# Attention and state-space encoder on one core: norm sums placed inside the input projection, head 0 prepared in separate banks, gate projection ended bank by bank

## The chip, the core and the metric
The kernel is one program on one core of one Trainium2 chip. The metric is the device time in microseconds of one execution. The core has TensorE for matrix products, whose results land in PSUM (eight banks of 512 f32 columns on 128 partitions), VectorE, ScalarE and GpSimd for everything else, and SyncE for most DMA issues. An engine takes its instructions in the order written; engines wait for each other by semaphores.

## The reference
An encoder with two layers runs over two sequences of 528 tokens (16 of them shared meta tokens), width 1024. Layer 0 mixes by attention with low-rank keys, values and queries, layer 1 by a chunked state-space scan; a gated feed-forward part follows each. The change touches these parts:

```python
def mla_mixer(u, w_in, q_norm, kv_norm, w_q_up, w_kv_up, q_head_norm, k_head_norm, w_out):
    c_q, c_kv, k_rope = jnp.split(u @ w_in, [Q_LORA_RANK, Q_LORA_RANK + KV_LORA_RANK], axis=-1)
    q = (rmsnorm(c_q, q_norm) @ w_q_up).reshape(b, L, MLA_HEADS, QK_HEAD_DIM)
    kv = (rmsnorm(c_kv, kv_norm) @ w_kv_up).reshape(b, L, MLA_HEADS, QK_NOPE_DIM + V_HEAD_DIM)
    k_nope, v = jnp.split(kv, [QK_NOPE_DIM], axis=-1)
    k = jnp.concatenate(
        [k_nope, jnp.broadcast_to(k_rope[:, :, None, :], (b, L, MLA_HEADS, QK_ROPE_DIM))], axis=-1)
    q, k = rmsnorm(q, q_head_norm), rmsnorm(k, k_head_norm)
    q, k = apply_rope(q, pos), apply_rope(k, pos)
    o = block_attention(q, k, v)
    return o.reshape(b, L, MLA_HEADS * V_HEAD_DIM) @ w_out

def ssd_mixer(u, w_in, conv_w, conv_b, dt_bias, a_log, d_skip, norm_w, w_out):
    z, xbc, dt_raw = jnp.split(u @ w_in, [D_INNER, D_INNER + CONV_DIM], axis=-1)
    ...
    y = y.reshape(b, L, D_INNER) * jax.nn.silu(z.astype(jnp.float32))
    y = rmsnorm(y, norm_w).astype(u.dtype)
    return y @ w_out
```

There are 16 heads with 64 plain and 32 rotated dimensions; the query rank is 384, the key-value rank 256. `z` has 2048 columns.

## The kernel before
All products are made in three parts: operand and weight are each split in a high and a low part (`Uhi`, `Ulo`, `Whi`, `Wlo`), and high x high, high x low and low x high are added in PSUM. GpSimd splits the weights (`Whi`, `Wlo`), two slots of them, one unit ahead of TensorE.

**Input projection (L852 to L858).** Six blocks of 128 output rows (m = 0 to 2 for the query rank, 3 and 4 for the key-value rank, 5 for the rotated key) go in turn to the bank groups 0 to 2 and 3 to 5. `product` runs eight steps (kt) of nine multiplications for each. ScalarE copies each block out, writes its high part and its squares; VectorE writes the low part and adds up the squares (`add_squares`, L1952) into SS for the input, SSQ[0] for the query rank and SSQ[1] for the key-value rank.

**Norm sums (L859 to L866).** Behind the projection TensorE sums the squares over the partitions by ten multiplications with one column each (`sums_by_part`, L826), four sets: SS, SSQ[0], SSQ[1] and the rotated key's squares SQ. VectorE then makes the norm factors of all tokens (TOK) in a chain of 45 small operations (L2032 to L2044), which ends with a signal `row_ready`. In between TensorE does the rotated key's pair product (L867 to L870, three multiplications of 352 columns), which gives it with its halves exchanged.

**Head 0 (L1024 to L1070).** Every product of the preparation uses one pair of banks, A_PREP = 5 and 6, and waits (`wait_prep`) until the engine that empties it has done so. The order is: two spreads of the rope factors over the partitions, K of both sequences, then the loop over j from -1 on. Its pass j = -1 has no scores, and prepares head 0 as each pass j >= 0 prepares head j + 1 between its own scores: Q (18 multiplications of 264 columns for each sequence), sums for the key norms and query norms, V in four parts (`V_PARTS`, 60 multiplications of 256 columns in all), two spreads of key factors. `prep_orders` numbers the uses of the pair, and ScalarE and VectorE count by these numbers (`prep_taken`, `stats_taken`). ScalarE empties Q and half of K and makes high parts; VectorE makes the factors, scales, turns the queries and makes low parts.

**Gate projection (L1272 to L1300).** Layer 1's `z` is made in four groups of 512 columns. A group fills all eight banks, one for each window of 128 tokens (w), over eight steps kt, two of them in each weight unit q:

```python
for kk in range(2):
    kt = 2 * q + kk
    for w in range(WIN):
        if kt == 0 and group_:
            pe.wait_ge(z_taken, (group_ - 1) * WIN + w + 1)
```

Each bank gets its last multiplication in the last step, and ScalarE empties the banks from 0 to 7 (`take_gates`, L1786 to L1795) by a Silu, ZB, which a DMA stores. Ahead of group 2 TensorE makes cumulative sums in banks 5 to 7, and ahead of group 3 exponent rows in banks 6 and 7; both wait for all eight banks. So does the scan that follows (L1304): its first products go to bank 5 (`products_bc`, tiles CCH and BCH), then to banks 0 to 3 (`decays`, tiles RH and LHS) and bank 4 (`chunk_state`, tiles XW and BTOK).

Every multiplication that is not a score or an output product is recorded with line L748, where the helper `mm` stands, so groups are told apart by their tiles.

## Time and profile before

| | us |
|---|---|
| median of three runs | 3419.45 |
| lowest and highest | 3417.31, 3433.54 |
| the profiled execution | 3425.27 |
| its span | 3423.5 |

| engine | busy, share of the span | instructions |
|---|---|---|
| PE (TensorE multiplications) | 3263.1 us, 95% | 19150 |
| PEld (weight loads) | 2945.2 us, 86% | 19150 |
| DVE (VectorE) | 1793.5 us, 52% | 2388 |
| ACT (ScalarE) | 791.0 us, 23% | 1395 |
| POOL (GpSimd) | 1258.4 us, 37% | 570 |

The mean granted clock of TensorE is 0.967 of its full 2.4 GHz; a stretch shows either 1.00 or 0.50, or a mixture where it holds both. Times of rows count from the start of the span. In a timeline a row is a run of like instructions: its start, its length, engine, line, operation, what it writes and reads, its shape and count, and in brackets the idle time of the engine before it, with what ended that.

### The profile page before, as it was taken

Reading aid. Unit: us, or ns where it says so; the run is one execution under the profiler, and the core shown is the slowest. Engines: PE = TensorE matmul, PEld = TensorE weight load, DVE = VectorE, ACT = ScalarE, POOL = GpSimd, SP = SyncE. Lnnn points to the kernel's source line nnn. Section 1 sums busy time; section 2 is a strip of 40 time slices with the busy share of each in tenths; the row PEclk is TensorE's granted clock in tenths of the full one; section 3 lists DMA queues with packets and bytes.
Section 4 is the critical chain, followed back from the end, with each engine's and each line's share of the span. In section 5 each row is a group of like instructions: output and inputs, shape, how many; then the busy total and the mean of one; then the engine's idle time right before and its main releaser. Section 6 shows DMA issues by size and latency. Waiting matters only on the chain.

```text
span 3423.5 us, 47898 instructions
## 1 busy us (share of the span) xinstructions
PE 3263.1 (95%) x19150; PEld 2945.2 (86%) x19150; DVE 1793.5 (52%) x2388; ACT 791.0 (23%) x1395; POOL 1258.4 (37%) x570
## 2 busy tenths in 40 slices
PE   7899999989999999999999999789998999999996
PEld 7799999989999999999999977566666788888885
DVE  4466666564333333334788842478888533333335
ACT  4165555461100000001211111233333100000001
POOL 4000000003444444444444343367673444444441
PEclk9699899899999999999999999899999999999998
DMA  2000000002111111111233422332323111111111
GB/s 107 19 12 9 14 5 14 14 19 82 44 43 43 47 45 43 45 47 44 92 93 93 134 74 99 103 103 92 110 92 111 43 48 44 49 44 48 49 47 57
DMA packets 112656, 198.66 MB, mean 58 GB/s; under 512 B 7413, under 2 KB 56821, under 8 KB 112501
## 3 DMA queue, kind: packets, MB, share of 16 engines
q1 hardware_dynamic: 71728, 146.82, 13.5%
q10 hardware_dynamic: 40773, 49.69, 4.3%
q8 instruction: 107, 1.75, 0.2%
q14 instruction: 48, 0.39, 0.0%
HBM read 161.10 MB, written 35.39 MB: 57 GB/s over the span
## 4 chain that ended last, share of the span: by engine, by line
PE 83%; DVE 7%; POOL 4%; issue 3%; ACT 2%; ACTq 1%; DMA 0%; DVEq 0%; POOLq 0%
PE PS L748 76%; PE PS L1019 4%; PE PS L1004 2%; POOL Wlo L669 1%; POOL SQ L714 1%; DVE SS L2261 1%; POOL RMS L679 1%; ACT ZB L1793 1%; DVE YC L2404 1%; PE PS L1209 1%; DVE SS L1952 0%; DVE H L2298 0%; DVE MX L2161 0%; PE PS L1346 0%; POOL SQ L709 0%
## 5 line engine op out<-in xcount | busy, mean ns | idle before, releaser
L626 POOL TENSOR_TENSOR Whi<-Wraw,const 128x1024 fp32r<-128x1024 f32 x186 | 451.7, 2428 | 1900.8 <-PE PS L748 1893.9
L748 PE MATMUL PS<-Uhi,Whi 128*128 128x352 f32 (+1 forms) x2504 | 620.3, 347 | 30.9 <-DVE Ulo L1964 19.3
L748 PE MATMUL PS<-Ulo,Whi 128*128 128x352 f32 (+1 forms) x2504 | 615.9, 346 | 0.0
L748 PE MATMUL PS<-Uhi,Wlo 128*128 128x352 f32 (+1 forms) x2504 | 614.3, 345 | 0.0
L629 POOL TENSOR_TENSOR Wlo<-Wraw,Whi 128x1024 fp32r<-128x1024 f32 x186 | 507.1, 2726 | 14.6
L748 PEld LDWEIGHTS PS<-Uhi,Whi 128*128 128x128 f32 x2504 | 440.1, 190 | 67.5 <-issue 18.7
L748 PEld LDWEIGHTS PS<-Ulo,Whi 128*128 128x128 f32 x2504 | 441.5, 189 | 31.3
L748 PEld LDWEIGHTS PS<-Uhi,Wlo 128*128 128x128 f32 x2504 | 440.8, 189 | 31.5
L2298 DVE TENSOR_TENSOR H<-H,PS 128x1056 f32<-128x1056 f32 (+1 forms) x176 | 217.5, 1237 | 264.8 <-PE PS L748 264.7
L2322 DVE TENSOR_TENSOR HID<-PS,RMS 128x1056 f32<-128x1056 f32 (+1 forms) x44 | 54.6, 1241 | 420.7 <-PE PS L748 420.2
L1703 ACT ACTIVATE HIDhi<-HID 128x1056 fp32r<-128x1056 f32 (+1 forms) x40 | 43.0, 1075 | 894.5 <-DVE HID L2327 894.5
L748 PE MATMUL PS<-HIDhi,Whi 128*128 128x352 f32 (+1 forms) x800 | 205.9, 355 | 5.3 <-DVE H L2298 5.3
L748 PE MATMUL PS<-HIDlo,Whi 128*128 128x352 f32 (+1 forms) x800 | 205.8, 355 | 0.0
L748 PE MATMUL PS<-HIDhi,Wlo 128*128 128x352 f32 (+1 forms) x800 | 205.7, 354 | 0.0
L2161 DVE TENSOR_REDUCE MX<-PS 106x1 f32<-106x528 f32 x160 | 113.1, 707 | 139.6 <-PE PS L748 138.3
L2404 DVE SCALAR_TENSOR_TENSOR YC<-XC,cols,YC 128x1052 f32<-128x1052 f32 (+1 forms) x96 | 180.8, 1883 | 3.4
L1019 PE MATMUL PS<-V,PT 106*106 106x64 f32 x1600 | 178.0, 261 | 0.5 <-ACT O L1605 0.5
L1019 PEld LDWEIGHTS PS<-V,PT 106*106 106x106 f32 x1600 | 170.4, 181 | 0.6 <-issue 0.6
L748 PEld LDWEIGHTS PS<-HIDhi,Whi 128*128 128x128 f32 x800 | 143.3, 190 | 20.7 <-DVE H L2298 6.0
L748 PEld LDWEIGHTS PS<-HIDlo,Whi 128*128 128x128 f32 x800 | 143.2, 190 | 14.9
L748 PEld LDWEIGHTS PS<-HIDhi,Wlo 128*128 128x128 f32 x800 | 142.9, 189 | 14.3
L2309 DVE TENSOR_TENSOR GATE<-PS,RMS 128x1056 f32<-128x1056 f32 (+1 forms) x43 | 53.4, 1241 | 191.1 <-PE PS L748 175.7
(288 smaller groups left out, 5369.0 us busy)
## 6 DMA issues: line engine op xcount, KB each, us to landing
Wraw<-in_w SPq DMA_DIRECT2D x211, 512.0 KB, 3.5
xt<-XTT ACTq DMA_DIRECT2D x20, 640.0 KB, 5.6
H<-in_x ACTq DMA_DIRECT2D x16, 528.0 KB, 7.9
Wraw<-in_w SPq DMA_DIRECT2D x32, 256.0 KB, 3.2
zt<-ZB ACTq DMA_DIRECT2D x32, 256.0 KB, 2.0
X<-xt SPq DMA_DIRECT2D x8, 1024.0 KB
Z<-zt SPq DMA_DIRECT2D x32, 256.0 KB, 2.6
saved<-H ACTq DMA_DIRECT2D x8, 528.0 KB, 7.4
```

The costliest lines, as they stand in the source:

```text
L626: pool.tensor_tensor(Whi[s][:], Wraw[s][:], ones.unsqueeze(1).broadcast_to([P, BLK, P]), ALU.mult)\
L629: pool.tensor_tensor(Wlo[s][:], Wraw[s][:], Whi[s][:].bitcast(F32), ALU.subtract)\
L669: pool.tensor_tensor(Wlo[s][:], Wraw[s][:], Whi[s][:].bitcast(F32), ALU.subtract)\
L748: ins = pe.matmul(out, lhsT, rhs, start=start, stop=stop, skip_group_check=True)
L1004: ins = pe.transpose(PS[0:CW, A_TURN + b // TURN_DVE, b % TURN_DVE * CW:(b % TURN_DVE + 1) * CW], PR[t % 2][:, key_start(b):key_start(b) + ...
L1019: ins = pe.matmul(PS[0:CW, A_OUT, 0:VD], PT[t % 2][:, b, :], V[x // 4 % 2][:, n // KB * KB + b, x // 2 % 2, x % 2 * VD:(x % 2 + 1) * VD], ...
L1703: act.activation(hi[:, k, 0:n], HID[:, 0:n], ACT.Copy).then_inc(hid_hi, c.adds(hid_hi))
L2161: step(vec.tensor_reduce(MX[:, t % RING:t % RING + 1], PS[0:CW, A_SCORE:A_SCORE + 2, 0:QHALF], AX_XY, ALU.max))
L2298: ins = vec.tensor_tensor(h, h, of(g), ALU.add)
L2309: vec.tensor_tensor(parted(GATE[:]), of(g), rms, ALU.mult)\
L2322: vec.tensor_tensor(parted(HID[:]), of(g), rms, ALU.mult)\
L2404: ins = vec.scalar_tensor_tensor(y_[:, :, to], x[:, :, of], taps[:, tap:tap + 1], y_[:, :, to], ALU.mult, ALU.add)
```

## The change
It has three parts.

**Norm sums.** The sets for SS, SSQ[0] and SSQ[1] are issued within the products of the fourth, fifth and sixth block (m = 3 and kt 0, m = 4 and kt 0, m = 5 and kt 4), in banks 6 and 7 in turn. VectorE's chain is cut: the part for the input norm stands in its loop behind block 2, the parts for query and key-value rank behind blocks 3 and 4. The tables of the rotation are loaded at the start, `trig_q` to its place and `trig_k` to the second half of KR, and `trig_q` is scaled behind block 0.

**Head 0.** Its preparation stands ahead of the loop, which begins with j = 0. K goes to banks 0, 1 and 2, 3; the rotated key's sums to bank 7; the pair product to banks 4 to 6; Q to banks 0, 1 and 2, 3; the rope spreads to 4, 5 and 2, 3; V to 6, 7, then 3, 4 and 2, 3, and 5, 6; the key spreads to 4, 5 and 0, 1. Five new semaphores carry what the counted uses carried. ScalarE's and VectorE's parts are written out in the same order.

**Gate projection.** The last unit of each group is done window by window, both steps of a window together, in the order 5, 6, 7, 0, 1, 2, 3, 4; ScalarE empties in that order. The waits for all eight banks become waits for the banks needed.

```diff
+ZORDER = (5, 6, 7, 0, 1, 2, 3, 4)
...
-    prep, stats = [("rope", s) for s in both] + [("k", 0, s) for s in both], []
-    for j in range(-1, HEADS - 1):
+    prep = [("k", 0, s) for s in both] + [("q", 0, s) for s in both] + [("v", 0, 0)]
+    prep += [("ks", 0, s) for s in both] + [("v", 0, i) for i in range(1, len(V_PARTS))]
+    stats = [("k", 0), ("q", 0)]
+    for j in range(HEADS - 1):
...
-    trig_k = RMS[:, 0:L]
+    trig_k = KR[1][:, 0:L]
...
+            def norm_sums(kt):
+                if (m, kt) in ((KQ, 0), (KQ + 1, 0), (KQ + KKV, 4)):
+                    k = m - KQ
+                    pe.wait_ge(sum_ready, c.want(sum_ready))
+                    sums_by_part(STAT_BANK + k % 2, k, (SS, *SSQ)[k], one).then_inc(stat_full, c.adds(stat_full))
+
+            product(group(m % 2), range(KD), Uhi, Ulo, range(KD), u_ready if m == 0 else None, norm_sums)\
                 .then_inc(to_scalar[m % 2], c.adds(to_scalar[m % 2]))
-        pe.wait_ge(sum_ready, c.want(sum_ready))
-        sums_by_part(STAT_BANK, 0, SS, one)
-        pe.wait_ge(sum_ready, c.want(sum_ready))
-        sums_by_part(STAT_BANK, 1, SSQ[0], one)
-        pe.wait_ge(sum_ready, c.want(sum_ready))
-        sums_by_part(STAT_BANK, 2, SSQ[1], one)
-        pe.wait_ge(rope_sq, c.want(rope_sq))
-        sums_by_part(STAT_BANK, 3, SQ, mask(M_ROPE)).then_inc(stat_full, c.adds(stat_full))
-        pe.wait_ge(rope_ready, c.want(rope_ready))
-        pe.wait_ge(grp_free[0], c.want(grp_free[0]))
-        for n in range(NB):
-            ins = mm(group(0)[:, n, :], pair_sum, CF[0][:, n * NT:(n + 1) * NT])
-        ins.then_inc(to_scalar[0], c.adds(to_scalar[0]))
         pe.wait_ge(u_ready, c.want(u_ready, KQ + KKV))
-        pe.wait_ge(row_ready, c.want(row_ready))
...
-        for g in range(2):
-            pe.wait_ge(grp_free[g], c.ahead(grp_free[g]))
+        pe.wait_ge(grp_free[0], c.ahead(grp_free[0]))
+        project_k(0, 0, 0)
+        pe.wait_ge(grp_free[1], c.ahead(grp_free[1]))
+        project_k(0, 1, 2)
+        pe.wait_ge(rope_sq, c.want(rope_sq))
+        sums_by_part(STAT_BANK + 1, 3, SSQ[1], mask(M_ROPE)).then_inc(stat_full, c.adds(stat_full))
+        pe.wait_ge(rope_ready, c.want(rope_ready))
+        for n in range(NB):
+            ins = mm(PS[:, 4 + n, 0:NT], pair_sum, CF[0][:, n * NT:(n + 1) * NT])
+        ins.then_inc(pair_full, 1)
+        pe.wait_ge(row_ready, c.want(row_ready))
+        key_norms(0, 0)
+        key_norms(0, 1)
         for s in range(NSEQ):
-            wait_prep("rope", s)
-            spread(s, TOK[:, K_RB, :])
-        for s in range(NSEQ):
-            project_k(0, s)
-        for j in range(-1, HEADS):
+            pe.wait_ge(prep_taken, PREP["k", 0, s] + 1)
+            pe.wait_ge(kr_taken, s + 1)
+            project_q(0, s, 0, 2 * s)
+            project_q(0, s, 1, 2 * s)
+        pe.wait_ge(pair_taken, 1)
+        spread(pair(4), 0, TOK[:, K_RB, :]).then_inc(rope_full, 1)
+        pe.wait_ge(prep_taken, PREP["q", 0, 1] + 1)
+        spread(pair(2), 1, TOK[:, K_RB, :]).then_inc(rope_full, 1)
+        project_v(0, 0, 6)
+        pe.wait_ge(rope_taken, 1)
+        spread_keys(0, 0, 4)
+        spread_keys(0, 1, 0)
+        query_norms(0, 0)
+        query_norms(0, 1)
+        pe.wait_ge(rope_taken, 2)
+        project_v(0, 1, 3)
+        project_v(0, 2, 2)
+        pe.wait_ge(prep_taken, PREP["ks", 0, 0] + 1)
+        project_v(0, 3)
+        for j in range(HEADS):
...
+        def z_matmul(w, kk, kt):
+
+            t = slice(window_start(w), window_start(w) + CK)
+            for p, (Xs, W) in enumerate(((Uhi, Whi), (Uhi, Wlo), (Ulo, Whi))):
+                ins = mm(PS[:, w, :], Xs[:, kt, t],
+                         W[now["slot"]][:, kk * HALF:(kk + 1) * HALF, :].rearrange("p m n -> p (m n)"),
+                         start=(kt == 0 and p == 0), stop=(kt == KD - 1 and p == 2))
+            return ins
+
+        def z_taken_from(group_, bank):
+
+            return group_ * WIN + ZORDER.index(bank) + 1
+
         for group_ in range(GROUPS):
             if group_ == 2:
-                pe.wait_ge(z_taken, 2 * WIN)
+                pe.wait_ge(z_taken, z_taken_from(1, 7))
                 cumulative_sums()
             if group_ == 3:
-                pe.wait_ge(z_taken, 3 * WIN)
+                pe.wait_ge(z_taken, z_taken_from(2, 7))
                 exponent_rows()
             for q in range(KD // 2):
                 enter_unit(V_Z + group_ * TILES_PER_GROUP + q)
+                if q == KD // 2 - 1:
+                    for w in ZORDER:
+                        z_matmul(w, 0, 2 * q)
+                        z_matmul(w, 1, 2 * q + 1).then_inc(z_full, 1)
+                    continue
                 for kk in range(2):
-                    kt = 2 * q + kk
                     for w in range(WIN):
-                        if kt == 0 and group_:
-                            pe.wait_ge(z_taken, (group_ - 1) * WIN + w + 1)
+                        if q == 0 and kk == 0 and group_:
+                            pe.wait_ge(z_taken, z_taken_from(group_ - 1, w))
                             if group_ == 2 and w > 4:
                                 pe.wait_ge(tab_taken, w - 4)
                             if group_ == 3 and w > 5:
                                 pe.wait_ge(rows_taken, 1)
-                        t = slice(window_start(w), window_start(w) + CK)
-                        for p, (Xs, W) in enumerate(((Uhi, Whi), (Uhi, Wlo), (Ulo, Whi))):
-                            ins = mm(PS[:, w, :], Xs[:, kt, t],
-                                     W[now["slot"]][:, kk * HALF:(kk + 1) * HALF, :].rearrange("p m n -> p (m n)"),
-                                     start=(kt == 0 and p == 0), stop=(kt == KD - 1 and p == 2))
-                        if kt == KD - 1:
-                            ins.then_inc(z_full, 1)
+                        z_matmul(w, kk, 2 * q + kk)
         now["release"], now["slot"] = now["slot"], None
-        pe.wait_ge(z_taken, GROUPS * WIN)
...
+        pe.wait_ge(z_taken, z_taken_from(3, 5))
         products_bc(0)
+        pe.wait_ge(z_taken, z_taken_from(3, 3))
         decays(0)
+        pe.wait_ge(z_taken, z_taken_from(3, 4))
         chunk_state(0, 0, 4)
...
+        for k in range(2):
+            act.dma_start(trig_q[:, k, :], trig_d[k]).then_inc(trig_in, 16)
...
+        act.activation(banks(CF[1][:]), group(1), ACT.Copy).then_inc(rope_raw, 1)
+        act.wait_ge(rope_raw, 1)
         act.sem_inc(grp_free[1], 1)
         act.wait_ge(sum_ready, c.want(sum_ready))
-        act.activation(SQ[:], CF[1][:], ACT.Square).then_inc(rope_sq, c.adds(rope_sq))
-        act.wait_ge(to_scalar[0], c.want(to_scalar[0]))
-        act.activation(banks(KR[0][NOPE:P, :]), group(0, parts=P - NOPE, at=NOPE), ACT.Copy)\
-            .then_inc(act_steps, c.adds(act_steps))
-        act.activation(banks(KR[1][0:P - NOPE, :]), group(0, parts=P - NOPE), ACT.Copy)\
-            .then_inc(grp_free[0], c.adds(grp_free[0]))
+        act.wait_ge(stat_full, c.want(stat_full, 3))
+        act.activation(SSQ[1][:], CF[1][:], ACT.Square).then_inc(rope_sq, c.adds(rope_sq))
         sq_by[0] = None
-        act.wait_ge(stat_full, c.want(stat_full))
-        for k in range(2):
-            act.dma_start(trig_q[:, k, :], trig_d[k]).then_inc(trig_in, 16)
-
-
-        halves = PS[:, A_PREP:A_PREP + 2, 0:QHALF]
+        c.want(stat_full)
...
+        for s in range(NSEQ):
+            take_k(0, s, 2 * s)
+        act.wait_ge(pair_full, 1)
+        act.activation(banks(KR[0][NOPE:P, :]), PS[NOPE:P, 4:7, 0:NT], ACT.Copy).then_inc(act_steps, c.adds(act_steps))
+        act.activation(banks(KR[1][0:P - NOPE, :]), PS[0:P - NOPE, 4:7, 0:NT], ACT.Copy).then_inc(pair_taken, 1)
+        for s in range(NSEQ):
+            take_q(0, s, 2 * s)
+        high_q(0)
+        high_k(0)
...
-            for w in range(WIN):
-                n = group_ * WIN + w
+            for i, w in enumerate(ZORDER):
+                n = group_ * WIN + i
...
+            if m == 0:
+                vec.wait_ge(trig_in, c.want(trig_in, 48))
+                for h in range(2):
+                    step(vec.tensor_scalar(trig_q[:, h, :], trig_q[:, h, :], col("q_head", h), None, ALU.mult))
+            if m == KQ - 1:
+                vec.wait_ge(stat_full, c.want(stat_full))
...
+            if m >= KQ:
+                k = m - KQ
+                rank, dst, dst2 = ((Q_RANK, K_A, K_A2), (KV_RANK, K_B, K_B2))[k]
...
+        step(vec.tensor_copy(tok(K_BV), tok(K_B)))
+        for w in range(KB - 1, KW, KB):
+            step(vec.tensor_tensor(TOK[:, K_BV, w:w + 1], TOK[:, K_B, w:w + 1], lower[0:CW, 2:3], ALU.mult))
+        vec.wait_ge(rope_raw, 1)
...
+        vec.wait_ge(rope_ready, c.given(rope_ready))
         for s in range(NSEQ):
-            scale_rope(s)
-        take_k(0, 0)
-        for j in range(-1, HEADS):
+            take_k(0, s, 2 * s)
+        vec.wait_ge(stat_full, c.want(stat_full))
+        step(vec.scalar_tensor_tensor(tok(K_RR), part_sum(STAT_BANK + 1, 3), 1.0 / QK, tok(K_R1SQ), ALU.mult, ALU.mult))
+        vec.sem_inc(row_ready, 1)
+        step(vec.tensor_scalar(tok(K_RR), tok(K_RR), EPS, None, ALU.add))
+        key_factors(0, 0)
+        key_factors(0, 1)
+        scale_rope(0, 4)
+        scale_rope(1, 2)
+        take_v(0, 0, 6)
+        turn_queries(0)
+        scale_keys(0, 0, 4)
+        scale_keys(0, 1, 0)
+        low_q(0)
+        low_k(0)
+        query_factors(0, 0)
+        take_v(0, 1, 3)
+        take_v(0, 2, 2)
+        query_factors(0, 1)
+        take_v(0, 3)
+        for j in range(HEADS):
```

Below, SS, SSQ and SQ are the sums of squares, CF the raw rotated key, TOK the factors by token, Chi and Clo the parts of the normed low-rank block.

TensorE, from the end of the input projection to the first products of head 0, before:

```order
L748 MATMUL PS<-const,SS 106x1 [waits sum_ready]
L748 MATMUL PS<-const,SS 106x1 x9
L748 MATMUL PS<-const,SSQ 106x1 [waits sum_ready]
L748 MATMUL PS<-const,SSQ 106x1 x9
L748 MATMUL PS<-const,SSQ 106x1 [waits sum_ready]
L748 MATMUL PS<-const,SSQ 106x1 x9
L748 MATMUL PS<-const,SQ 106x1 [waits rope_sq]
L748 MATMUL PS<-const,SQ 106x1 x9
L748 MATMUL PS<-CF,const 128x352 [waits grp_free0,rope_ready]
L748 MATMUL PS<-CF,const 128x352 x2
L748 MATMUL PS<-const,TOK 128x106 [waits grp_free0,grp_free1,row_ready,u_ready]
```

TensorE, from the last K product of head 0 to its first Q product, after:

```order
L757 MATMUL PS<-Clo,Whi 128x264 x2
L757 MATMUL PS<-Chi,Wlo 128x264 x2
L757 MATMUL PS<-const,SSQ 106x1 [waits rope_sq]
L757 MATMUL PS<-const,SSQ 106x1 x9
L757 MATMUL PS<-CF,const 128x352 [waits rope_ready]
L757 MATMUL PS<-CF,const 128x352 x2
L757 MATMUL PS<-const,SS 106x2 [waits k_squared,row_ready]
L757 MATMUL PS<-const,SS 106x2 x9
L757 MATMUL PS<-Chi,Whi 128x264 [waits kr_taken,prep_taken]
L757 MATMUL PS<-Chi,Whi 128x264
```

Three of the four sets of sums have left this place, K stands ahead of the remaining set and Q behind the key norms; the spreads come later and wait for `pair_taken` and `prep_taken` alone.

VectorE, at the fourth block of the projection, before:

```order
L2020 SCALAR_TENSOR_TENSOR Clo<-CF,cols,Chi 128x1056 [waits hi_ready]
L1952 TENSOR_TENSOR SSQ<-SSQ,SQ 128x1056 [waits sq_free,sq_full]
L2020 SCALAR_TENSOR_TENSOR Clo<-CF,cols,Chi 128x1056 [waits hi_ready]
L1949 COPY SSQ<-SQ 128x1056 [waits sq_full]
L2020 SCALAR_TENSOR_TENSOR Clo<-CF,cols,Chi 128x1056 [waits hi_ready]
L1952 TENSOR_TENSOR SSQ<-SSQ,SQ 128x1056 [waits sq_free,sq_full]
L2027 SCALAR_TENSOR_TENSOR CF<-CF,cols,RMS 128x1056 [waits u_ready,trig_in,rope_sq]
L2032 TENSOR_SCALAR TOK<-PS 106x10 [waits stat_full]
L1975 TENSOR_SCALAR TOK<-TOK 106x10 [waits vec_steps]
```

VectorE, at the third to the fourth block, after:

```order
L2065 SCALAR_TENSOR_TENSOR Clo<-CF,cols,Chi 128x1056 [waits hi_ready]
L1997 TENSOR_TENSOR SSQ<-SSQ,SQ 128x1056 [waits sq_free,sq_full]
L2074 TENSOR_SCALAR TOK<-PS 106x10 [waits stat_full]
L2020 TENSOR_SCALAR TOK<-TOK 106x10 [waits vec_steps]
L2023 TENSOR_SCALAR TOK<-TOK 106x10 [waits vec_steps]
```

The chain's first operation, which stood behind the rope product of CF, now stands behind the squares of the third block.

TensorE, where the gate projection ends and the scan begins, before:

```order
L748 MATMUL PS<-Whi,Ulo 128x512
L748 MATMUL PS<-CCH,BCH 128x128 [waits hg_in0,z_taken]
L748 MATMUL PS<-CCH,BCH 128x128 x3
L748 MATMUL PS<-RH,LHS 128x512 [waits rh_in0,hg_in0]
L748 MATMUL PS<-RH,LHS 128x512 x3
L748 MATMUL PS<-XW,BTOK 128x512 [waits xw_ready,hg_in0]
```

The same place, after:

```order
L757 MATMUL PS<-Whi,Ulo 128x512
L757 MATMUL PS<-CCH,BCH 128x128 [waits hg_in0,z_taken]
L757 MATMUL PS<-CCH,BCH 128x128 x3
L757 MATMUL PS<-RH,LHS 128x512 [waits rh_in0,hg_in0,z_taken]
L757 MATMUL PS<-RH,LHS 128x512 x3
L757 MATMUL PS<-XW,BTOK 128x512 [waits xw_ready,hg_in0,z_taken]
```

The order is the same; one wait for all banks has become three for the banks of each product.

## Rows read from the trace of the kernel before

**Rows 1.** Chain of waits, shares of the span by engine (part 4).
```profile
PE 83%; DVE 7%; POOL 4%; issue 3%; ACT 2%; ACTq 1%; DMA 0%; DVEq 0%; POOLq 0%
```

**Rows 2.** Timeline of TensorE, projection's end to scores: start, us, instructions.
```profile
93.86 1.94 PE L748 MATMUL PS<-const,SS 128*106 128x1 f32 x20
...
100.65 3.74 PE L748 MATMUL PS<-const,SQ 128*106 128x1 f32 x20
104.25 3.87 PE L748 MATMUL PS<-CF,const 128*128 128x352 f32 x6
...
165.99 0.56 PE L748 MATMUL PS<-KHI,QHI 128*106 128x264 f32 x2
```

**Rows 3.** Waits of TensorE, 94 to 166: total us, how many, longest.
```profile
PE PS L748 <- DVEq L2045: 5.6, 1, 5.6
PE PS L748 <- DVE KR L2069: 3.2, 2, 1.6
```

**Rows 4.** Windows, TensorE: stretch, length, busy (count), granted clock, DMA, GB/s.
```profile
113.70:142.40 28.70, 22.22 (x99) 0.50 0.06 19
142.40:149.20 6.80, 5.68 (x51) 1.00 0.00 0
```

**Rows 5.** Timeline of TensorE at the gate projection's four group borders.
```profile
2014.87 0.47 PE L748 MATMUL PS<-Whi,Uhi 128*128 128x512 f32 x1 [2.25 <-ACT ZB L1793]
...
2066.75 1.02 PE L748 MATMUL PS<-A,const 128*128 128x320 f32 x4 [3.91 <-ACT ZB L1793]
...
2121.56 1.45 PE L1269 MATMUL PS<-const,KT 128*128 128x128 f32 x8 [3.91 <-ACT ZB L1793]
...
2172.93 1.71 PE L748 MATMUL PS<-CCH,BCH 128*128 128x128 f32 x8 [3.91 <-ACT ZB L1793]
```

**Rows 6.** Windows, TensorE, columns as in rows 4.
```profile
872.90:876.30 3.40, 3.40 (x13) 0.50 0.48 154
...
2067.50:2074.30 6.80, 6.80 (x21) 0.50 0.11 41
2122.20:2125.50 3.30, 3.30 (x12) 0.50 0.21 79
...
374.00:397.80 23.80, 23.80 (x126) 0.51 0.01 2
```

**Rows 7.** Timeline of TensorE, first feed-forward part.
```profile
869.34 2.29 PE L748 MATMUL PS<-const,SS 128*128 128x1 f32 x20
```

**Rows 8.** Timeline of VectorE, additions of squares.
```profile
33.77 1.26 DVE L1952 TENSOR_TENSOR SS<-SS,SQ 128x1056 f32<-128x1056 f32 x1
...
86.11 3.44 DVE L1952 TENSOR_TENSOR SSQ<-SSQ,SQ 128x1056 f32<-128x1056 f32 x1
```

**Rows 9.** Timeline of VectorE, first and last of the 45 small operations.
```profile
104.43 0.17 DVE L2032 TENSOR_SCALAR TOK<-PS 106x10 f32<-106x10 f32 x1 [6.76 <-PE PS L748]
...
113.42 0.17 DVE L2044 SCALAR_TENSOR_TENSOR TOK<-PS,TOK 106x10 f32<-106x10 f32 x1
```

**Rows 10.** Chain that ended last: start, us, work (part of it).
```profile
113.75 2.88 PE PS L748 x12
...
127.30 2.99 PE PS L748 x12
...
131.88 11.36 PE PS L748 x56
...
149.68 2.87 PE PS L748 x12
...
160.74 5.46 PE PS L748 x24
```

**Rows 11.** Window, TensorE, third group of the gate projection; columns as in rows 4.
```profile
2140.00:2160.00 20.00, 20.00 (x88) 1.00 0.50 166
```

**Rows 12.** Timeline of ScalarE, first and last Silu of the first group.
```profile
2014.04 0.69 ACT L1793 ACTIVATE ZB<-PS,RT 128x512 f32<-128x512 f32 x1
...
2021.95 0.69 ACT L1793 ACTIVATE ZB<-PS,RT 128x512 f32<-128x512 f32 x1 [0.46 <-ACT ZB L1793]
```

119 lines of the change are left out of this document (55 added, 64 removed).

## The prediction

> **What bounds the kernel now.** I read the chain of waits first. TensorE carries 83% of it [rows 1], so time can only go where TensorE stands idle, where it runs at its lower clock, or where it is given less work. The change gives it the same number of multiplications (the instruction lists of both kernels hold the same sets), so only idle time and clock count.
>
> The timeline of TensorE between the input projection and the first scores is the first place. The projection ends at 93.86, where the norm sums begin, and the first score product starts at 165.99 [rows 2]: 72.1 us in which no attention is done. The list of waits of that stretch is headed by one of 5.6 us behind VectorE's norm chain; next come two of 1.6 us behind the scaling of the rope keys [rows 3], then smaller ones of the same kind, behind whoever empties the one pair of banks. In all it is about 16 us of the 72. The rest is work, most of it slow: the clock is at 0.50, the 1.2 GHz level, from 113.7 to 142.4, and at 1.00, 2.4 GHz, only from 142.4 to 149.2 [rows 4]. Both belong together. TensorE falls to the lower level after sums with one column each and after waits, and gets back after some dense products without a gap.
>
> The second place is the gate projection. At each of its group borders the timeline of TensorE shows a wait for ScalarE's gate evictions: 2.25 us before 2014.87, 3.91 before 2066.75, 3.91 before 2121.56 and 3.91 before 2172.93 [rows 5]. After each the clock is down for a while: 6.8 us after the second, 3.3 us after the third [rows 6].
>
> **Norm sums inside the projection: a cost of 3.4 us on the path, bounds 0 and 5.1.** Three sets of ten sums move to between products of the projection. At the full clock a set costs 1.94 us [rows 2], so the projection becomes 5.8 us longer; the same sets leave the stretch behind it. What is new is the clock. The trace has one such set amid dense products, in the first feed-forward part: 2.29 us from 869.34 [rows 7], and the clock is at 0.50 from 872.9 to 876.3 [rows 6]. Dense work of 3.4 us at half speed loses 1.7 us. Three sets lose between nothing and 5.1; I take two of three, 3.4. The projection then ends at 93.86 + 5.8 + 3.4 = 103.1. The last set needs the squares of the fifth block summed: its last addition ends 3.44 us after 86.11, at 89.55 [rows 8], 7.2 us after that block's product; five of eight steps of an 11.7 us product are 7.3 us, so the wait is about nothing.
>
> VectorE's chain of 45 small operations (104.43 to 113.42, [rows 9]) is cut in three. Each of the first two parts costs about 3 us behind an addition of squares, where VectorE otherwise waits for the next block. The third, about 4 us with the V factors, runs during the last three steps of the projection. Only the rope term and the key factors stay behind. So the 5.6 us wait goes, and what is late next is TensorE itself. The rotation tables are loaded at the start (two more ACT issues, before ScalarE has its first input) and scaled in the projection while VectorE waits for the second block: nothing.
>
> **Head 0 in separate banks: 40.4 us instead of 72.1.** Each consumer now has its own banks, so TensorE goes on with the next product while ScalarE and VectorE empty the last. What remains is TensorE's own work. At the lower clock it costs, from the timeline and the chain [rows 2, 10]: K 2 x 2.99 = 6.0; rope sums 3.74; rope pair product 3.87; key norms and all of Q 11.36; two rope spreads 2 x 2.88 = 5.8; V, 60 multiplications at 5.46 / 24, 13.7; two key spreads 2 x 2.87 = 5.7; query norms as the rope sums, 3.7. The sum is 53.8 us; at the full clock half of it, 26.9. These two are the bounds. Between them the clock decides. The order is K (dense), sums, pair product, norms, Q (dense), spreads, V, spreads, norms, V (dense, 48 multiplications). I expect the clock to fall at the first sums and norms, rise within Q, fall again by the query norms and rise in the last V: about half the work at each level, 40.4 us. The first scores then start at 103.1 + 40.4 = 143.5 instead of 165.99, a gain of 22.5.
>
> Do the other engines keep up? The durations that follow are from VectorE's timeline, too many for rows, its small steps 0.2 us each with their handover [rows 9]. At the full clock, the tightest case: the key factors (two parts of about 1.5 us) run under 4 us of Q; the rope scaling (2 x 1.4 us) ends while TensorE does the first V; then VectorE has V 0.7, the turn of Q 1.25, key scalings 1.4, low parts 2.5, query factors 3.0 and V 1.4, some 10 us against 11 us of TensorE. ScalarE has less. There is little room, but TensorE stays last.
>
> A cost of the move lies in GpSimd. The V weights are split as soon as the projection ends instead of behind the first rope spread, now beside VectorE's rope product. An addition of two SBUF tensors takes 1.26 us alone (33.77) and 3.44 us beside GpSimd's split (86.11) [rows 8]. The rope product would then be ready some 4.6 us after the projection's end; TensorE reaches the product that needs it after K and the rope sums, 3.0 + 1.9 = 4.9 us at the full clock. So it costs nothing here, 2 us if TensorE came earlier. The Trainium skill, GPSIMD Engine Reference, section 1. Specifications, says that GpSimd shares VectorE's SBUF interfaces and contends with instructions that have two SBUF inputs; by that rule VectorE's step lengthens by the 2.2 us of the rows and the sum stays.
>
> **Gate projection bank by bank: a gain of 15.0 us, bounds 9 and 18.** A multiplication of 512 columns takes 20 / 88 = 0.23 us [rows 11], so in the last unit each bank is now finished 1.4 us after the one before. ScalarE needs (2021.95 - 2014.04) / 7 = 1.13 us per bank [rows 12], so it keeps pace, and seven of eight banks are taken when TensorE is done. Borders one by one:
> - second (2066.75): the 4.1 us of idle time go and the clock stays up, 6.8 / 2 = 3.4: 7.5 us.
> - third (2121.56): 3.9 + 3.3 / 2 = 5.6 us. The exponent rows go to banks 6 and 7, freed first; the copy that ScalarE and VectorE make of them takes 2.3 us and is wanted about 4 us later.
> - last: TensorE begins the scan's products at once, 3.9 us earlier, and part of a slow stretch goes: 4.4 us. VectorE clears a table and weighs two tiles (2.5 us) before the third product; TensorE gets there after 3 us.
> - first: a loss. ScalarE comes late there, at 2014.04, after its exponentials, and takes all eight banks in one row until 2022.65. Before, it starts with bank 0, which TensorE wants first. Now bank 0 is the fourth: 2014.04 + 3 x 1.13 + 0.7 = 2018.1. Bank 4 is the eighth, free at 2022.65, and banks 5 to 7 stand behind it on TensorE: 3 x 0.7 = 2.1 us more than before, when bank 7 came last. All at the lower clock it is 4.9. I take 2.5, near the low end, since a rise of the clock is due after some dense work.
>
> Together 7.5 + 5.6 + 4.4 - 2.5 = 15.0.
>
> **Sum.** 22.5 + 15.0 = 37.5 us. The profiled execution took 3425.27 us (span 3423.5) and becomes 3387.8. The median of the runs shown, 3419.45, lies 5.8 us below it; the same gain gives 3382.
>
> **Rivals.**
> A, the waits go but the clock does not come back: all of head 0's preparation at 1.2 GHz, 53.8 us instead of 40.4, and all three sets cost: 15 us less gain, 3397. For it: the 28.7 us at 0.50 with TensorE busy for 22.2 of them [rows 4]. Against it: there it waited in between. The Trainium skill, TensorE: Matmul & The Clock Gate, section A second HAM failure mode: psum-queue depth-cycling, warns that short idle times between groups in changing banks make the clock go up and down; it would give this case.
> B, the clock stays up throughout: 26.9 us and no loss in the projection, 3365. It needs sums and spreads to count as enough work; the rows at 872.9 speak against that.
> C, slower: the heads run in a pattern in which TensorE is busy without a gap and still stays at the lower level for 23.8 us (374.0 to 397.8, [rows 6]), a loss of 12 us. Where the pattern falls against the clock changes with the start of the scores. One such stretch more gives 3394. From four on the kernel is slower than before, and five eat 60 us: 3419 - 37 + 60 = 3442. Nothing suggests five.
> D, the change does not do what it says: new waits stand for the old, because VectorE is the last in the preparation or ScalarE falls behind in the last gate unit. Half of the gain lost: 3401.
>
> **Chances.** The forecast 0.56 (its own range 3370 to 3394), A 0.18, B 0.13, C 0.03, D 0.10. The range takes in A and B and leaves out C and part of D: 3361 to 3403. A difference under 0.5% (17 us) can hardly be told from none here. Faster by more than that needs less than 3402: 0.92; within: 0.06; slower: 0.02.
>
> **What would show it.** The first score product near 143 (135 to 155); one wait at most over 1 us between projection and scores; sets of sums inside the fourth, fifth and sixth block's products, with 0.50 behind one or two; a table of the clock in which the preparation has both levels. At the gate borders no wait for ScalarE at the second, third and fourth, and a longer one, 5.5 us, at the first, with a first pass that ends 2 us later. I am wrong if TensorE waits for VectorE behind the query factors, if the clock is at one level throughout, or if the heads' own stretch changes by more than 12 us.

## The result

| | us |
|---|---|
| before, median of 4 runs | 3423.21 (3417.31 to 3433.54) |
| after, median of 4 runs | 3369.54 (3365.41 to 3374.71) |
| ratio after to before | 0.9841, 95% interval 0.981 to 0.9871 |
| the profiled execution after | 3374.71, span 3372.9 |
| forecast | 3382, range 3361 to 3403 |

The kernel is 1.6% faster: 53.7 us by the medians, 50.6 us by the spans of the two profiled executions (3423.5 and 3372.9). The forecast was 37.5. The direction and the range held, and the excess has one place, the preparation of head 0. The time is nearly that of rival B (3365 us, chance 0.13), not that of the forecast proper.

The first of the two places is the preparation of head 0. The timeline of TensorE in the kernel after answers to [rows 2] (start, us, instructions):

```profile
60.61 1.94 PE L757 MATMUL PS<-const,SS 128*106 128x1 f32 x20
...
74.18 1.94 PE L757 MATMUL PS<-const,SSQ 128*106 128x1 f32 x20
...
93.69 2.03 PE L757 MATMUL PS<-const,SSQ 128*106 128x1 f32 x20
...
100.05 0.40 PE L757 MATMUL PS<-Chi,Whi 128*128 128x264 f32 x2
...
102.97 2.02 PE L757 MATMUL PS<-const,SSQ 128*106 128x1 f32 x20
104.85 2.02 PE L757 MATMUL PS<-CF,const 128*128 128x352 f32 x6
106.71 1.94 PE L757 MATMUL PS<-const,SS 128*106 128x2 f32 x20
...
112.99 2.82 PE L757 MATMUL PS<-const,TOK 106*128 106x106 f32 x24
...
127.24 0.40 PE L757 MATMUL PS<-KHI,QHI 128*106 128x264 f32 x2
```

The projection ends at 100.05 and the first score product starts at 127.24: 27.2 us of preparation for 72.1. The rope sums and the pair product, 3.74 and 3.87 us before, take 2.02 each. The windows show why, beside [rows 4] (stretch, length, busy and count, granted clock, DMA, GB/s):

```profile
94.00:127.20 33.20, 33.20 (x280) 1.00 0.09 31
```

TensorE is busy for all of it and the clock is at 1.00, the 2.4 GHz level, throughout.

The second place is the gate projection. The timeline of TensorE at its borders, for [rows 5]; the last three rows have no brackets, since nothing was waited for ahead of them:

```profile
1979.95 0.76 PE L757 MATMUL PS<-Whi,Uhi 128*128 128x512 f32 x1 [5.58 <-ACT ZB L1838]
...
2026.49 0.87 PE L757 MATMUL PS<-A,const 128*128 128x320 f32 x4
...
2073.83 1.03 PE L1298 MATMUL PS<-const,KT 128*128 128x128 f32 x8
...
2119.44 1.05 PE L757 MATMUL PS<-CCH,BCH 128*128 128x128 f32 x8
```

The three waits of 3.91 us are gone, and the first border has one of 5.58 instead of 2.25. Behind it the same form takes 0.63 us for some 3 us where it takes 0.39 later: the clock is down there too.

Where the 50.6 us of the two traces lie, by the starts of the same instructions:

| from | to | before | after | gain |
|---|---|---|---|---|
| start | first score product | 166.0 | 127.2 | 38.8 |
| first score product | last | 589.9 | 595.4 | -5.5 |
| last score product | first gate product | 1211.7 | 1206.8 | 4.9 |
| first gate product | scan | 205.4 | 190.1 | 15.3 |
| scan | end | 1250.6 | 1253.5 | -2.9 |

The rows for the three stretches that the change doesn't touch differ mainly in how much of them ran at the lower clock. In the heads' loop it is 71.7 us after and some 65 before, which costs about 3 of the 5.5 us; TensorE's idle time there also rose, from 17.4 to 19.1 us. The stretch ahead of the gate projection, for instance, holds a piece of 10.2 us at 0.50 before, and one of 3.4 at the same work after (windows, first of before, then of after):

```profile
1664.80:1675.00 10.20, 10.20 (x47) 0.50 0.57 216
```

```profile
1635.00:1638.40 3.40, 3.40 (x13) 0.52 0.50 154
```

The median fell by 53.7 where the traces say 50.6; single executions of a kernel differ by as much as that.

### The profile page after: what moved, and what is told of

Same layout as the page of the kernel before. It is cut to its first block, busy times and chain, and to the rows that moved or that the text cites. A ratio compares the mean times of both kernels' runs of the same rounds, so it can differ in the third digit from the quotient of the medians.

```text
span 3372.9 us, 47877 instructions
## 1 busy us (share of the span) xinstructions
PE 3236.7 (96%) x19150; PEld 2923.6 (87%) x19150; DVE 1791.2 (53%) x2388; ACT 790.9 (23%) x1395; POOL 1260.2 (37%) x570
## 4 chain that ended last, share of the span: by engine, by line
PE 84%; DVE 7%; POOL 4%; issue 3%; ACT 1%; ACTq 0%; DMA 0%; DVEq 0%; POOLq 0%
PE PS L757 77%; PE PS L1023 4%; PE PS L1008 2%; POOL Wlo L678 1%; POOL SQ L723 1%; POOL RMS L688 1%; DVE SS L2324 1%; DVE YC L2467 1%; PE PS L1238 1%; DVE SS L1997 0%; DVE H L2361 0%; DVE MX L2205 0%; PE PS L1385 0%; POOL SQ L718 0%; DVE Ulo L2433 0%
## 5 line engine op out<-in xcount | busy, mean ns | idle before, releaser
L757 PEld LDWEIGHTS PS<-Uhi,Whi 128*128 128x128 f32 x2504 | 439.8, 189 | 66.4 <-issue 17.3
L757 PEld LDWEIGHTS PS<-HIDhi,Wlo 128*128 128x128 f32 x800 | 143.1, 190 | 14.4
```

Source lines behind the costliest of these rows:

```text
L757: ins = pe.matmul(out, lhsT, rhs, start=start, stop=stop, skip_group_check=True)
```

## The experiments

Times below are medians with the ratio to the kernel before and its interval. The kernel before took 3423.0 us beside the parts alone, 3428.1 beside the sums three times, the queries through one pair, the norms apart and the first group in order, and 3429.1 beside the rest; across these groups the ratios compare, the medians only to some us. The trace has two records for each norm sum and each piece of a spread, so x20 is a set of ten sums and x12 six pieces; where the expectations speak of ten, twenty, twelve or sixty products of these kinds, they count records. A window that begins a few tenths of a us after the clock has fallen takes in a little of the full clock behind it, so a stretch wholly at 0.50 can read up to 0.57.

### The parts alone

**Gate projection alone.** The kernel before with the gate part of the change:

```diff
+                if q == KD // 2 - 1:
+                    for w in ZORDER:
+                        z_matmul(w, 0, 2 * q)
+                        z_matmul(w, 1, 2 * q + 1).then_inc(z_full, 1)
+                    continue
...
-        pe.wait_ge(z_taken, GROUPS * WIN)
```

> The kernel before with the gate projection of the change alone. The traces of before and after give 205.3 us against 190.0 from the first gate product (1967.6, 1929.4) to the first product of the scan (2172.93, 2119.44), so this part should be worth 15 us by itself: ratio 0.9955, and the same 5.6 us wait at the first border. Rival: part of the 15 us is a better clock that comes with the shifted start of the stage; then the stretch takes 195 us or more here, and the ratio is 0.997 or above.

Measured: 3412.77 us, ratio 0.9969 (0.9956 to 0.9982). From the first gate product at 1968.77 to the scan at 2159.65 its trace takes 190.9 us, after took 190.1 and before 205.4. So the 15 us stand by themselves in the trace, and don't come from the start of the stage. The spans of the two traces differ by 14.4 us, the medians by 10.2; the interval of the ratio is 6 to 15 us, with the trace's value at its edge.

**Attention part alone.** The kernel after with the old gate projection:

```diff
-                if q == KD // 2 - 1:
-                    for w in ZORDER:
...
+        pe.wait_ge(z_taken, GROUPS * WIN)
```

> The kernel after with the gate projection of before. The first score product should start at 127.2 as in after, 38.8 us earlier than before; the gain in time is that or a few us less, since the heads' own stretch took 5.3 us more in the trace of after: 33 to 39 us, ratio 0.9885 to 0.9905. Rival: the two parts help each other, and this one gives 42 us or more.

Measured: 3383.63 us, ratio 0.9875 (0.9856 to 0.9894). By the medians it gains 39.4 us, just above the 33 to 39 expected, and the ratio's interval is 36 to 49. The scores start at 130.3, 3.1 us later than in after: 6.8 us from 121.1 on ran at the lower clock, behind the key spreads and query norms. The two parts add within the noise: 39.4 and 10.2 are 49.6, after gained 53.7.

**Sums inside alone.** Attention part cut further: sums in the projection, chain in three, but head 0 in the loop's pass j = -1 through banks 5 and 6:

```diff
-        project_k(0, 0, 0)
-        pe.wait_ge(grp_free[1], c.ahead(grp_free[1]))
-        project_k(0, 1, 2)
...
+            wait_prep("rope", s)
+            spread(pair(A_PREP), s, TOK[:, K_RB, :]).then_inc(prep_full, 1)
+        for s in range(NSEQ):
+            project_k(0, s)
+        for j in range(-1, HEADS):
```

> The kernel before with the norm sums inside the projection and VectorE's chain cut in three, but head 0 through the one pair of banks, with its waits, and the old gate projection. Theory 1: the clock falls behind sums and spreads that stand in a row, and idle time behind the one pair of banks does not lower it. Then only the rope sums are left in a row with nothing, the clock stays up over most of the stretch, and the scores start at 26.9 us of work and 10 us of waits behind the projection's end at 99.7: 137 to 145. Theory 2: it is the idle time at the banks that keeps the clock down. Then only the wait of 5.6 us goes and the slow stretches stay: scores at 155 to 162.

Measured: 3421.2 us, ratio 0.9983 (0.9968 to 0.9998), scores at 162.6, 0.6 us past the range of theory 2, and nearly nothing gained. The waits of TensorE from 94 to 160 (total us, how many, longest) and windows of the same trace:

```profile
PE PS L755 <- DVE KR L2074: 3.2, 2, 1.6
PE PS L755 <- DVE KR L2082: 3.2, 2, 1.6
PE PS L755 <- ACT SSQ L1520: 2.7, 1, 2.7
PE PS L755 <- ACT KR L1524: 2.4, 1, 2.4
```

```profile
105.30:108.70 3.40, 3.30 (x6) 0.57 0.00 0
112.10:139.40 27.30, 20.85 (x96) 0.51 0.07 20
146.20:162.60 16.40, 13.89 (x60) 0.50 0.00 1
```

The 5.6 us wait for the chain in [rows 3] is gone, and two others, of 2.7 and 2.4 us, stand in its place: for ScalarE's squares and its copy of the pair product, which the chain had hidden. And the clock stays at the lower level for 47 us, as long as the waits at the banks go on. Theory 1 as written fails. But the spreads, the rope sums and the norms still stand between the waits here, so this run doesn't show that the waits alone do it.

**Banks alone.** The kernel with separate banks, the sums in a row behind the projection, the chain in one piece behind the rope sums:

```diff
+        for k in range(3):
+            pe.wait_ge(sum_ready, c.want(sum_ready))
+            ins = sums_by_part(STAT_BANK + 1, k, (SS, *SSQ)[k], one)
+        ins.then_inc(stat_full, c.adds(stat_full))
```

> The kernel after with the three sets of sums in a row behind the projection, VectorE's chain of 45 operations behind the rope sums, head 0 in separate banks, old gate projection. TensorE waits some 7 us for the chain before the key norms, which start near 114 instead of 106.7. Theory 1 (sums in a row lower the clock): the clock is at its lower level from about 98, and 20.5 us of work behind the key norms take 30 or more; scores at 142 to 155. Theory 2 (idle time behind the banks lowers it): one wait of 7 us costs at most one short slow stretch, scores at 135 to 139.

Measured: 3391.77 us, ratio 0.99 (0.9878 to 0.9921), though its profiled execution took 3407.96, the longest of its runs; scores there at 147.9. Both theories have a part in it. Timeline and windows of TensorE:

```profile
94.10 1.94 PE L757 MATMUL PS<-const,SS 128*106 128x1 f32 x20
95.90 5.95 PE L757 MATMUL PS<-const,SSQ 128*106 128x1 f32 x40
...
120.73 3.76 PE L757 MATMUL PS<-const,SS 128*106 128x2 f32 x20 [9.53 <-DVEq L2221]
```

```profile
97.90:108.10 10.20, 10.20 (x55) 0.52 0.18 49
115.00:128.70 13.70, 7.96 (x42) 0.52 0.00 0
138.90:145.70 6.80, 6.80 (x36) 0.54 0.00 0
```

The clock falls first within three sets of sums in a row, with TensorE busy for all 10.2 us, and again in the wait of 9.5 us. By the traces, sums inside alone give 3.4 us at the scores, banks alone 18.1, both together 35.7 to 38.8 (130.3 and 127.2). In these traces the parts help each other by some 15 us. By the medians they gain 1.8, 31.2 and 39.4 us, a surplus of 6 us with an uncertainty as large. The traces show that each half alone still leaves long stretches at the lower clock (47 us and 31 us); how large the surplus is on an average execution, and whether there is one, stays open.

### What lowers the clock

**Sums three times.** Each of the three sets in the projection is issued three times:

```diff
+                    for again in range(2):
+                        sums_by_part(STAT_BANK + k % 2, k, (SS, *SSQ)[k], one)
                     sums_by_part(STAT_BANK + k % 2, k, (SS, *SSQ)[k], one).then_inc(stat_full, c.adds(stat_full))
```

> The kernel after with each of the three sets of sums in the projection issued three times: 60 one-column products in a row between dense ones, with no idle time. Extra work 3 x 2 x 1.94 = 11.6 us at the full clock. Theory 1 (a row of such products lowers the clock by itself): a slow stretch behind each of the three, the projection's end at 113 or later. Theory 2 (only idle time lowers it): no slow stretch, and the end at 100.05 + 11.6 = 111.7, everything behind as in after.

Measured: 3389.0 us, ratio 0.9899 (0.9874 to 0.9923). Timeline and windows of TensorE:

```profile
60.80 7.65 PE L757 MATMUL PS<-const,SS 128*106 128x1 f32 x60
...
82.82 5.90 PE L757 MATMUL PS<-const,SSQ 128*106 128x1 f32 x60
...
107.60 6.90 PE L757 MATMUL PS<-const,SSQ 128*106 128x1 f32 x60
```

```profile
64.40:74.60 10.20, 10.20 (x45) 0.51 0.16 51
82.80:88.30 5.50, 5.50 (x61) 0.98 0.01 1
88.30:91.70 3.40, 3.40 (x14) 0.53 0.24 77
112.20:119.00 6.80, 6.80 (x29) 0.51 0.01 2
```

Each triple set is followed by a stretch at the lower level, and TensorE is busy in all of them. The projection ends at 120.83, 9.1 us later than the 111.7 that the work alone gives; half of 10.2 + 3.4 + 6.8 is 10.2. (The execution in this trace, 3377.86 us, is the fastest of its four: of the 20.8 us lost up to the projection's end it gets back 16 in the heads' loop, which ran 37.5 us at the lower level here and 71.7 in after.) So a row of one-column products lowers the clock with no idle time at all. A single set of 1.94 us between dense products mostly doesn't: the nine traces with the sums placed as in the change show a fall behind the third set in two (at 96.3 and 97.3, 3.4 us each), and none behind the first or second. "Mostly" holds for this place only: behind the single set of [rows 7] in the first feed-forward part the clock fell for 3.4 us in ten of the fourteen traces of this case. That set takes 2.29 us and these 1.94 to 2.03; why the places differ isn't shown.

**Queries through one pair of banks.**

```diff
-            project_q(0, s, 0, 2 * s)
-            project_q(0, s, 1, 2 * s)
+            if s:
+                pe.wait_ge(prep_taken, PREP["q", 0, 0] + 1)
+            project_q(0, s, 0, 0)
+            project_q(0, s, 1, 0)
```

> The kernel after with the queries of both sequences of head 0 through banks 0 and 1, so that TensorE waits once, about 1.6 us, for ScalarE between two dense blocks of 18 products. If a single short wait at the banks lowers the clock, the stretch behind 112 is slow and the scores start 8 us or more later than 127.2. If it takes several in a row, or waits next to sums and spreads, they start 1.6 us later, at 128.8, and the time is that of after within 3 us.

Measured: 3370.71 us, ratio 0.9818 (0.9789 to 0.9848), with single executions from 3353.9 to 3376.9; the wait is 0.79 us, the scores start at 128.6. The window of TensorE:

```profile
94.00:128.60 34.60, 33.81 (x283) 1.00 0.10 31
```

The clock stays up and the time is that of after, as expected for a single short wait that lowers nothing.

**K and Q through one pair of banks.** The same for K (`project_k(0, 1, 0)`, behind waits for both takers of the first K).

> The kernel after with K and Q of both sequences of head 0 through banks 0 and 1. TensorE waits for the first K (VectorE's part comes behind its rope product, so some 4 us) right ahead of the rope sums, pair product and key norms, and twice in Q, 3 us in all. Theory (idle time next to small products lowers the clock, though a wait between dense products did not): a slow stretch of 10 us or more behind 104, scores at 139 or later. Rival (idle time alone costs only itself): scores at 127.2 + 6 = 133 to 135.

Measured: 3381.26 us, ratio 0.9862 (0.9844 to 0.9879); the waits are 2.76 and 0.79 us, the scores start at 134.2. Windows of TensorE:

```profile
104.50:107.90 3.40, 3.31 (x18) 0.54 0.46 154
107.90:128.40 20.50, 19.71 (x170) 0.99 0.00 1
128.40:131.80 3.40, 3.40 (x19) 0.54 0.00 0
```

The rival's range holds: the waits cost themselves, 3.6 us, and half of two stretches of 3.4 us at the lower level, 7.0 later in all. The first of them is new and begins in the wait of 2.76 us. The second lies behind the key spreads and query norms, where five traces without these waits (the attention part alone, the sums three times, the norms apart, the first group in order, both edits) have one too. Neither one short wait nor two holds the clock down. What keeps it down for long, in the kernel before and with the sums inside alone, is one wait after another, ten and eleven of 0.7 us and more from the projection's end to the scores, with sums and spreads between. Which share the waits and which the small products have there wasn't separated; that this is the reason for the long slow stretches of the preparation is argued from it, not shown apart.

### A second place where the clock falls

In the trace of after, each of the seven slow stretches of the heads' loop begins at the same work: the query norms of an even head, 20 records with one column, and the 12 of a key spread behind them (timeline of TensorE):

```profile
252.81 1.06 PE L1023 MATMUL PS<-V,PT 106*106 106x64 f32 x10
253.70 1.98 PE L757 MATMUL PS<-const,SQ 128*106 128x1 f32 x20
255.54 2.57 PE L757 MATMUL PS<-const,KS 106*128 106x106 f32 x12
257.80 0.75 PE L757 MATMUL PS<-KHI,QHI 128*106 128x264 f32 x2
```

The same work stands there in every trace without the norms apart: seven places in each of ten traces. The clock fell at 59 of these 70, 1.7 to 3.6 us after the norms began, and nowhere else in the loop. The pair of score products that takes 0.41 us elsewhere takes 0.75 behind it, and the window says 0.50 for 17 us:

```profile
256.00:273.10 17.10, 17.10 (x87) 0.50 0.00 1
```

**Norms apart.** One edit in TensorE's order, on top of after:

```diff
-                    if n == 5:
-                        query_norms(nxt, 0)
-                        query_norms(nxt, 1)
                     if 5 <= n < 7:
+                        query_norms(nxt, n - 5)
                         spread_keys(nxt, n - 5)
```

> The kernel after, and in the heads' loop one thing more: for each even head the two sets of query norms (ten one-column products each) no longer stand together ahead of a key spread, but one in each of two query windows, as they do for odd heads. In the trace of after every slow stretch of the loop starts at that place (184.3, 256.0, 337.9, 409.6, 491.5, 563.2, 645.1), 71.7 us in all. Theory 1: twenty one-column products and twelve of 106 columns in a row are what lowers the clock there; then less than 25 us of the loop are slow, and the time is 20 to 30 us shorter than after, about 3345. Theory 2: the clock falls there for other reasons (the score pattern itself, the 0.6 us waits for ScalarE); then the slow time stays within 15 us of 71.7 and the time at 3370.

Measured: 3341.02 us, ratio 0.9746 (0.973 to 0.9762): 28.5 us under after by the medians, 32 by the ratios, more than half of what the whole change gained, for an edit of three lines. The windows of the heads' loop, first of after, then of this kernel:

```profile
127.20:722.60 595.40, 576.30 (x5081) 0.94 0.03 11
```

```profile
130.40:692.50 562.10, 542.71 (x5081) 1.00 0.04 11
```

The loop with the same 5081 records takes 33.3 us less, and no slow stretch is left. The other three traces with the norms apart have none either (561.9 to 562.2 us), while the ten without spend 37.5 to 78.5 us at the lower level and take 579.6 to 596.3. So the one trace is not a lucky one. The place itself (timeline):

```profile
255.28 1.04 PE L757 MATMUL PS<-const,SQ 128*106 128x1 f32 x10
256.19 1.56 PE L757 MATMUL PS<-const,KS 106*128 106x106 f32 x12
257.53 0.47 PE L757 MATMUL PS<-KHI,QHI 128*106 128x264 f32 x2
...
259.68 1.04 PE L757 MATMUL PS<-const,SQ 128*106 128x1 f32 x10
```

Half of the 71.7 us at the lower clock is 35.9, and 33.3 came back. The short waits for ScalarE, which theory 2 named, are still there: 17.9 us in 31 waits over the loop, 17.3 in 29 before the edit. They don't lower the clock by themselves.

**The same edit on the kernel before.**

> The kernel before, with one edit: the two sets of query norms of even heads apart, as in the earlier run on the kernel after. If this gain needs nothing of the change, the heads' loop goes from 590 to 562 us here too, and the ratio is 0.990 to 0.992; head 0's preparation, which this edit touches as well, may give some us more. If the change is needed for it, less than 15 us.

Measured: 3398.01 us, ratio 0.9907 (0.9888 to 0.9926). The loop takes 562.2 us (164.7 to 726.9), and the gain is 31.1 us by the medians. It needs nothing of the change.

**First gate group in the order 0 to 7**, on top of after:

```diff
+def zorder(group_):
+    return ZORDER if group_ else tuple(range(WIN))
...
-                    for w in ZORDER:
+                    for w in zorder(group_):
```

> The kernel after, with the first gate group emptied in the order 0 to 7, the other three as in the change. ScalarE comes late to that group in any order, and bank 0 is wanted first: the wait at the first border goes from 5.6 to 2.3 us as before, with smaller ones behind it (0.24 and 0.19), so 2 to 3 us less in the stretch from the first gate product to the scan (190.0 to 187.5). Rival: the later banks become free at the same time as before, and what is saved at bank 0 is waited for at banks 5 to 7: no gain. The difference is under what the times can tell; the trace decides.

Measured: 3368.26 us, ratio 0.982 (0.9801 to 0.984). Timeline of TensorE at the first border:

```profile
1972.14 0.47 PE L762 MATMUL PS<-Whi,Uhi 128*128 128x512 f32 x1 [2.30 <-ACT ZB L1843]
...
1976.47 0.50 PE L762 MATMUL PS<-Whi,Uhi 128*128 128x512 f32 x1 [0.17 <-ACT ZB L1843]
```

The wait is 2.30 again, with four of 0.2 us behind it, and the stretch takes 188.1 us (1924.8 to 2112.9) for 190.1: 2 us, by the traces alone. The other traces agree: the three with the old order in the first group give 188.0 to 188.1 us, the six with the new order there 190.1 to 191.1.

**Both edits, and one more in head 0.** The combined kernel has the norms apart and the first group in order; the last kernel also moves the second V part ahead of head 0's query norms:

```diff
-        query_norms(0, 0)
-        query_norms(0, 1)
         pe.wait_ge(rope_taken, 2)
         project_v(0, 1, 3)
+        query_norms(0, 0)
+        query_norms(0, 1)
```

> The kernel after with the query norms of even heads apart in the loop and the first gate group emptied in the order 0 to 7: both edits that gained by the trace. They lie 1200 us apart, so they should add: 33 us in the loop (595.4 to 562 us) and 2 us in the gate projection; about 3338 to 3340, ratio 0.974. Rival: a shifted start lets the clock fall elsewhere and eats part of it, 3345 or more.

> As the combined kernel, and in head 0's preparation the second V part (12 products of 256 columns) stands between the key spreads and the query norms. In three of six traces with separate banks and sums inside, a slow stretch of 3.4 to 6.8 us began right behind these spreads and norms (121.4, 122.0, 124.1). If rows of small products lower the clock, none begins there now: 1.7 us, no more than the trace can show. Rival: VectorE gets its query factors 1.5 us later and TensorE waits for it ahead of the scores; then the first score comes later than in the combined kernel.

Measured: 3340.15 us, ratio 0.9739 (0.9724 to 0.9754), and 3339.19 us, ratio 0.9739 (0.9725 to 0.9754). The loop takes 561.9 us in both, the gate stretch 188.0 in the first. The combined kernel has its piece at the lower clock at 122.2, the last one has none there, and its scores start at 129.0 too, since it has one at 97.3. One trace without such a piece shows little, since the kernel after and the one with the queries through one pair have none there either. No time can be told between them, or from the one with the norms apart alone (3341.02). All three beat both kernels of this case by far; the best is 2.6% under before.

## Why the prediction was right, and where it was off

The time fell in the range and half of the mechanism held: the waits went as said. The other half, the clock, came out otherwise, and the prediction's own signs say so. It named as a sign of being wrong "if the clock is at one level throughout", which is what the trace shows, and the first score product, expected between 135 and 155, came at 127.2. The range held because it took in rival B. By chance the error also looks smaller than it was: the 5.5 us lost in the heads, which had no term in the sum, stand against the 16.3 us by which the gain of the preparation was put too low.

**The bound.** TensorE's idle time and clock were all that counted. Its chain share rose from 83% to 84%:

```profile
PE 84%; DVE 7%; POOL 4%; issue 3%; ACT 1%; ACTq 0%; DMA 0%; DVEq 0%; POOLq 0%
```

**Norm sums inside.** Three sets of 1.94 to 2.03 us, as forecast. The loss of clock was put at 3.4 us from the feed-forward set in [rows 6, 7]; it was 0 in this trace, the lower bound, and 1.7 in two of nine. The projection ended at 100.05, not 103.1. The last set's wait was nothing, as forecast: VectorE's addition ran from 90.20 to 93.64 and the sums began at 93.69.

**Head 0: the failed term.** The forecast was 40.4 us, half at each level; it took 27.2 (bound: 26.9). The gain at the scores was 38.8 instead of 22.5. The work list was right to 0.3 us; the step that failed is "I expect the clock to fall at the first sums and norms, rise within Q, fall again by the query norms": in this trace it fell at none of them. In four other traces with the same preparation (the attention part alone, the norms apart, the first group in order, both edits) it fell there once, by the query norms, for 3.4 or 6.8 us. The row that misled was the set in the feed-forward part, taken as what one set does everywhere; there the clock falls in ten of fourteen traces, in the projection behind two of 27 sets. The runs also show that the length of three sets in a row lowered the clock at each of three places, and that a preparation with waits in close succession stays at the lower level even when three of its sums are taken out of it. So rival B was right for the preparation, and A (waits gone, clock not back) wasn't. The Trainium skill, TensorE: Matmul & The Clock Gate, section A second HAM failure mode: psum-queue depth-cycling, names frequent short idle times at changing banks as the cause of an unsteady clock. The trace with the sums inside alone agrees (47 us at the lower level beside eleven waits of 0.8 to 2.7 us); the one with a single wait of 0.79 us and no fall isn't a case of it. The falls in the sums three times, with TensorE busy throughout, are something else.

**Other engines keep up.** Right: not one wait of TensorE between projection and scores. Rival D fell.

**GpSimd beside the rope product.** Mis-sized: the product was put at 3.44 us and took 1.48 (VectorE's timeline after):

```profile
101.40 1.48 DVE L2095 SCALAR_TENSOR_TENSOR CF<-CF,cols,KR 128x1056 f32<-128x1056 f32 x1 [1.81 <-ACT CF L1551]
```

GpSimd's split did run beside it and was the one that paid: its low part took 2.17 us instead of 1.34 (GpSimd's timeline after):

```profile
101.85 2.17 POOL L662 TENSOR_TENSOR Wlo<-Wraw,Whi 128x512 fp32r<-128x512 f32 x1
```

It had no effect on the end, as said, with more room than said. What the sum missed is who starts first. The addition of [rows 8] starts at 86.11, after GpSimd's low part (85.15 to 88.44), and ends 1.1 us behind it; here VectorE starts first (101.40 to 102.88) and GpSimd ends 1.1 us behind VectorE. The kind of operation is not the reason: the same kind as the rope product, started after GpSimd's, took 3.41 us for its usual 1.31 (timelines of GpSimd, then VectorE, before):

```profile
15.58 2.70 POOL L629 TENSOR_TENSOR Wlo<-Wraw,Whi 128x1024 fp32r<-128x1024 f32 x1
```

```profile
15.99 3.41 DVE L1964 SCALAR_TENSOR_TENSOR Ulo<-H,cols,Uhi 128x1056 fp32r<-128x1056 f32 x1
```

**Gate projection.** Forecast and measured, border by border, from the starts in [rows 5] and their answers above:

| border | forecast | measured | working |
|---|---|---|---|
| first | -2.5 | -1.8 | 95.3 without the next wait, now 97.1 |
| second | 7.5 | 7.5 | wait 3.9, pass 50.9 to 47.3 |
| third | 5.6 | 5.8 | wait 3.9, pass 47.5 to 45.6 |
| last | 4.4 | 3.9 | the wait |
| sum | 15.0 | 15.3 | |

The wait at the first border was forecast at 5.5 and is 5.58. Of the last border's 4.4, the 0.5 for "part of a slow stretch" doesn't show: the first 73.1 us of the scan have a mean granted clock of 0.77 before and after.

**Rival C**, that the heads' own pattern falls otherwise against the clock, took about 3 of the loop's 5.5 us: it ran 71.7 us at the lower level instead of some 65. That isn't a fixed cost of the change: in the six other traces with separate banks and the loop unchanged it ran 37.5 to 78.5 us at that level. "Nothing suggests five" such stretches held; that the pattern could be broken by moving five sums of each even head wasn't seen.

**The sum.** 37.5 against 50.6 in the traces: 16.3 more in the preparation, 0.3 more in the gate projection, 5.5 less in the heads, 2.0 more in stretches that the change doesn't touch.

## What to carry to other kernels

Look where each stretch at the lower clock begins, and at what TensorE did just before: here it was rows of one-column sums and spreads, and preparations with one wait after another. Moving five sums to the next query window was worth 28.5 us, close to the 31.2 us of the separate banks for head 0. Where waits and rows of small products stand together, try taking both away: the sums' move gained 1.8 us alone and 8.2 (39.4 less 31.2) with the separate banks, though this difference is no larger than its uncertainty.

A bank-wise end of a long accumulation hid the eviction entirely where the evictor kept pace (1.13 us against 1.4 here), but not at the border where the evictor came late; there the old order was better by 2 us.
